# Delta rule's decay and step size rows: ten fp32 products with ones become twenty single-pass products on high and low parts

## The chip, the cores and the metric

The kernel runs on one core of a Trainium2 chip. The metric is the device time in microseconds of one execution; 955.31 us is the median of three runs of the kernel before. Names of engines: PE is TensorE, ACT is ScalarE, DVE is VectorE, POOL is GpSimd, SP is SyncE.

## The reference, cut to what matters

One inference step of one layer: a hybrid mixer (gated delta rule, a short convolution, stick-breaking attention), memory cross-attention and a convolutional feed-forward, for 512 prompt tokens and 8 samples of 16 tokens. The change lies in the gated delta rule. Of each chunk:

```python
gc = jnp.cumsum(g, axis=-1)
diff = gc[..., :, None] - gc[..., None, :]
decay = jnp.exp(jnp.where(causal, diff, -jnp.inf))
kk = jnp.einsum('bhtd,bhsd->bhts', k, k)
L = jnp.where(strict, beta[..., None] * kk * decay, 0.0)
qk = jnp.einsum('bhtd,bhsd->bhts', q, k) * decay
o = jnp.einsum('bhtk,bhkv->bhtv', q * jnp.exp(gc)[..., None], S) + ...
```

`diff` needs, for every token of a tile, the cumulated decay of every other token, and `L` the step size beta: values that stand one to a partition (a column) have to stand along the free dimension in every partition (a row).

## The kernel before

The 640 tokens are five tiles (NT) of 128: four of the prompt (PT = 4) and one of the eight samples. Each engine runs one program in order; semaphores tie them together. All the large weight products are already made from high and low parts in a format that PE handles in a single pass (F32R): `whi`, `wlo`, `hhi`, `hlo`; the small ones are fp32.

After the projections of q, k and v, each tile i goes through these steps.

- ACT, `decay_source(i)` (L1795): for each of four heads the triangle of ones is scaled by the decay `gdec` into `rsrc[i % 2][0]` (L1799), and the identity by the log of q's norm into `qdiag` (L1801).
- DVE, `query_norm(i)` (L2328): the sum of both, L2330.
- PE, `decay_rows(i)` (L780): two products with 4 columns (the cumulated decay as columns, bank gcol), then ones times `rsrc[..][0]`, 512 columns, L789: every partition gets the row of cumulated decays (bank grow).
- PE, `key_products(i)`: kk and qk, 128x128 for each head, L796.
- POOL, `beta_source(i)` (L1495): the identity times the step size `ratio`, L1498; PE, `beta_rows(i)`: ones times that, L803 (bank brow).
- DVE, `decay_part(i)`: small columns (L2364 to L2370), then the differences from bank grow (L2376); ACT takes two Exp (L1838 from DVE's differences, L1842 from the bank); POOL, `decays(i)`, masks with the triangle (L1485).
- DVE, in its loop: qk and kk times the decay (L2395, L2397), the next tile's `query_norm(i + 2)`, L times the beta row (L2402), q times its Exp (L2405), a transpose of the tile before (L2383).

PE's order is four fill units, `decay_rows(0)`, `key_products(0)`, `decay_rows(1)`, `beta_rows(0)`, and then for each tile i from 1: a fill unit, `decay_rows(i + 1)`, `key_products(i)`, `beta_rows(i)`. A fill unit is 24 single-pass products of 320 columns of another projection (L495 to L497), there to keep PE at work while the others prepare. ACT's order is `decay_source(0)`, an Exp for the ratio, `decay_source(1)`, `z_out(2)`, and then for each tile: small Exps, the two Exps, `decay_source(i + 2)`, `z_out(3 + i)` (a fill unit's bank to SBUF), `blocks_out(i - 1)`. The buffers of sources are two deep, so `decay_source(i + 2)` waits for L789 of tile i. After the last tile come the level products (L837, L843), which solve the triangular system.

Of the kernel before, what the change touches and what calls it, by code (L numbers as in the profile page):

```python
# [67 lines left out]
def hybrid_step(nc, A, O):  # L68
    ctx = ExitStack()
    with ctx:  # L70
        at_r5 = [R5]

        def at(name, shape, offset, dt=F32):
            return nc.alloc_sbuf_tensor_at(name, shape, dt, offset=offset)

        def keep(name, shape, dt=F32):
            n = 4
            for s in shape[1:]:
                n *= s
            t = at(name, shape, at_r5[0], dt)  # L80
            at_r5[0] += (n + 31) // 32 * 32
            return t
# [4 lines left out]
        def spread(ap, axis, shape):  # L87
            return ap.unsqueeze(axis).to_broadcast(shape)
# [35 lines left out]
        apart_q, apart_w = [at("apart_q", [P, 2, HEADS, P], R1), at("apart_w", [P, 2, HEADS, P], R1 + 2 * TILE)]  # L124
        smp_vn, smp_o = [at(f"smp{n}", [P, HEADS, P], R1 + TILE * (4 + n)) for n in range(2)]

        rsrc = [[at(f"rsrc{n}{m}", [P, HEADS, P], CQ + TILE * (2 * n + m)) for m in range(2)] for n in range(2)]

        sqG = [at(f"sqG{n}", [P, TOK], CQ + TOK * 4 * n) for n in range(2)]
        rG = [at(f"rG{n}", [P, TOK], KT + TOK * 4 * n) for n in range(2)]  # L130
# [66 lines left out]
        junk3 = at("junk3", [P, D_MODEL], at_r5[0] - 2 * 2688)  # L197
        ident = keep("ident", [P, P])
        ones = keep("ones", [P, P])
        uptri = keep("uptri", [P, P])  # L200
        up16 = keep("up16", [P, P])
        same16 = keep("same16", [P, P])
        same64 = keep("same64", [P, P])
        lmask = keep("lmask", [P, LEVELS, P])
        at_ones = at_r5[0] - (5 + LEVELS) * P * 4
        T_AT = {"gate": (R0, R0 + 6144), "up": (RF, at_ones)}
        traw = {n: at(f"traw_{n}", [P, 3, half_block, P], o[0]) for n, o in T_AT.items()}
        tlo = {n: at(f"tlo_{n}", [P, 3, half_block, P], o[0], F32R) for n, o in T_AT.items()}
# [15 lines left out]
        def lane(name, *dims):  # L224
# [16 lines left out]
        lnr = keep("lnr", [P, NT, HEADS, 2])  # L241
        pick = keep("pick", [P, 64])
        ratio = keep("ratio", [P, NT, HEADS])
        gown = keep("gown", [P, HEADS, DEC_BATCH])
        kdec = keep("kdec", [P, NT, HEADS])
        bege = keep("bege", [P, NT, HEADS])
# [17 lines left out]
            "eps_ready", "ident_ready", "consts", "small_loaded", "gains_loaded", "w_first", "w_first_lo", *[f"x_loaded{n}" for n in range(X_PARTS)], "ones_ready", "xhi_ready", "xlo_ready", "sqx_ready", "sqs_ready", "rx_ready",  # L264
            "hf_ready", "hhi_ready", "hlo_ready", "mrow_loaded", "memT_loaded", "mem_hi", "mem_lo", "mk_rstd", "pz_ready", "rstd_ready", "xn_ready", "h_hi_ready",
            "w_hi_ready", "w_lo_ready", "w_lo_dve", "w8_ready", "add4_ready", "kstep", "conv_done", "cq_zeros", "sig_ready", "silu_done", "sq_ready",
            "l2_ready", "ratio_act", "ratio_ready", "decay_row", "decay_src", "beta_src", "gates", "gates_act", "dif_ready", "dt_ready", "dtu_ready", "small_exp",
            "lt_ready", "xt0_ready", "xb_ready", "xt_zero", "lb_ready", "lm_ready", "kd_ready", *[f"v_cache_loaded{n}" for n in range(DEC_BATCH)],
            *[f"k_cache_loaded{n}" for n in range(DEC_BATCH)], "yb_ready", "apart_zero", "apart_ready", "A_ready", "q_blocks", "past_ready", "st_loaded", "vm_ready", "sqf_ready", "rf_ready", "y_ready",
            "yhi_ready", "ylo_ready", "xres_loaded", "gm_loaded", "f_loaded", "qroot_ready", "qscale_ready",  # L270
# [5 lines left out]
        def flat(t):  # L276
            return t[:, :, :].rearrange("p a b -> p (a b)")
# [28 lines left out]
        def tri(i):  # L306
            return uptri if i < PT else up16
# [122 lines left out]
        def _(pe):  # L430
# [12 lines left out]
            def done(ins, key):  # L443
                ins.then_inc(bank_full[use[key][0]], 1)
# [332 lines left out]
                    scores(scored)  # L777

            ring[0] = "gdn"
            def decay_rows(i):  # L780
                b = take(("gcol", i))
                T.matmul(bank[b][:, 0:4], (uptri if i < PT else up16)[:, :], gdec[:, i, :], start=True, stop=True)
                if i == PT:
                    T.matmul(bank[b][:, 8:8 + HEADS * DEC_BATCH], ones[:, :], flat(gown), start=True, stop=True)
                done(T.matmul(bank[b][:, 4:8], (ones if i < PT else same16)[:, :], gdec[:, i, :],
                              start=True, stop=True), ("gcol", i))
                pe.wait_ge(s["decay_src"], i + 1)
                b = take(("grow", i))
                done(T.matmul(bank[b][:, :], ones[:, :], flat(rsrc[i % 2][0]), start=True, stop=True), ("grow", i))  # L789

            def key_products(i):
                tt = slice(i * P, (i + 1) * P)
# [7 lines left out]
            def beta_rows(i):  # L800
                pe.wait_ge(s["beta_src"], i + 1)
                b = take(("brow", i))
                done(T.matmul(bank[b][:, :], ones[:, :], flat(rsrc[i % 2][1]), start=True, stop=True), ("brow", i))  # L803

            for n in range(4):
                fill()
# [579 lines left out]
        def _(pool):  # L1386
# [3 lines left out]
            def link(ins):  # L1390
                chain[0] += 1
                ins.then_inc(s["pool_chain"], 1)
                pool.wait_ge(s["pool_chain"], chain[0])
# [32 lines left out]
            for t, v in ((newm, 0.0), (own8, 1.0), (same16, 1.0)):  # L1426
# [15 lines left out]
                     channel_multiplier=-1))  # L1442
            sel(out=own8[:, :], in_=own8[:, :], compare_op=ALU.is_ge, fill=0.0, base=DEC_SEQ - 1,
                pattern=[[DEC_SEQ, DEC_BATCH]], channel_multiplier=-1)
            link(G.memset(pick[:, :], 0.0))
            G.memset(pick[:, 32:33], 1.0)
            G.tensor_copy(lmask[:, 0, :], ident[:, :])
# [47 lines left out]
            def beta_source(i):  # L1495
                if i >= 2:
                    filled(pool, ("brow", i - 2))
                G.tensor_tensor(rsrc[i % 2][1][:, :, :], spread(ident[:, :], 1, [P, HEADS, P]),  # L1498
                                spread(ratio[:, i, :], 2, [P, HEADS, P]), ALU.mult).then_inc(s["beta_src"], 1)

            pool.wait_ge(s["ratio_ready"], 1)
            filled(pool, ("z", NI - 1, 0))
            beta_source(0)
            beta_source(1)
            decays(0)
# [66 lines left out]
        def _(act_e):  # L1572
# [222 lines left out]
            def decay_source(i):  # L1795
                if i >= 2:
                    filled(e, ("grow", i - 2))
                for h in range(HEADS):
                    V(rsrc[i % 2][0][:, h, :], tri(i)[:, :], ACT.Copy, scale=gdec[:, i, h:h + 1])  # L1799
                for h in range(HEADS):  # L1800
                    ins = V(qdiag[i % 2][:, h, :], ident[:, :], ACT.Copy, scale=lnr[:, i, h, 0:1])  # L1801
                ins.then_inc(s["decay_row"], 1)

            evacuated(e, ("gates", 2))
            e.wait_ge(s["gates_act"], 1)
# [10 lines left out]
            e.wait_ge(s["l2_ready"], 1)  # L1816
            decay_source(0)
            V(ratio[:, :, :], ratio[:, :, :], ACT.Exp, scale=-0.5).then_inc(s["ratio_act"], 1)
            decay_source(1)
            z_out(2)  # L1820

            def blocks_out(i):
# [5 lines left out]
            for i in range(NT):  # L1828
                evacuated(e, ("gcol", i))
                V(kdec[:, i, :], gcs[:, i, 2, :], ACT.Exp)  # L1830
                V(bege[:, i, :], gcs[:, i, 3, :], ACT.Exp)
                if i < PT:
                    ins = V(etot[:, i, :], gcs[:, i, 1, :], ACT.Exp)
                else:
                    ins = V(etotS[:, :, :], etotS[:, :, :], ACT.Exp)
                ins.then_inc(s["small_exp"], 1)
                e.wait_ge(s["dif_ready"], i + 1)
                V(scr[4 + i % 2][:, :, :], scr[4 + i % 2][:, :, :], ACT.Exp).then_inc(s["dt_ready"], 1)  # L1838
                if i >= 2:
                    e.wait_ge(s["lt_ready"], i - 1)  # L1840
                b = filled(e, ("grow", i))
                V(scr[6 + i % 2][:, :, :], quad(b), ACT.Exp).then_inc(bank_free[b], 1)  # L1842
                if i + 2 < NT:
                    decay_source(i + 2)
                z_out(3 + i)
                if i >= 1:
                    blocks_out(i - 1)
                if i == 3:
                    cut_hi(B_SB)
            cut_hi(B_OUT[0][0])  # L1850
# [276 lines left out]
        def _(dve):  # L2127
# [199 lines left out]

            def query_norm(i):  # L2328
                dve.wait_ge(s["decay_row"], i + 1)
                V.tensor_tensor(rsrc[i % 2][0][:, :, :], rsrc[i % 2][0][:, :, :], qdiag[i % 2][:, :, :], ALU.add)                    .then_inc(s["decay_src"], 1)  # L2330

            for u, (name, i, c, h) in enumerate(UNITS):
                ct = (u - 8) // 2
# [14 lines left out]
                if h == 1 and ct >= 1:  # L2348
# [5 lines left out]
            query_norm(0)  # L2354
            dve.wait_ge(s["ratio_act"], 1)
            V.scalar_tensor_tensor(out=ratio[:, :, :], in0=ratio[:, :, :], scalar=DK ** 0.5, in1=beta[:, :, :],
                                   op0=ALU.mult, op1=ALU.mult).then_inc(s["ratio_ready"], 1)
            query_norm(1)
            dve.wait_ge(s["out_sb"], 64)

            passed(dve, ("av", NI - 1))
# [23 lines left out]
            decay_part(0)  # L2385
            for i in range(NT):
                tt = slice(i * P, (i + 1) * P)
                if i + 1 < NT:
                    decay_part(i + 1)
                dve.wait_ge(s["small_exp"], i + 1)  # L2390
                V.tensor_tensor(bege[:, i, :], bege[:, i, :], beta[:, i, :], ALU.mult)
                dve.wait_ge(s["dtu_ready"], i + 1)
                d = scr[8 + i % 2][:, :, :]
                b = filled(dve, ("qk", i))
                V.tensor_tensor(qkD[i][:, :, :], quad(b), d, ALU.mult).then_inc(bank_free[b], 1)  # L2395
                b = filled(dve, ("kk", i))
                V.tensor_tensor(LT[i][:, :, :], quad(b), d, ALU.mult).then_inc(bank_free[b], 1)  # L2397
                if i + 2 < NT:
                    query_norm(i + 2)
                evacuated(dve, ("kk", i))  # L2400
                b = filled(dve, ("brow", i))
                V.tensor_tensor(LT[i][:, :, :], LT[i][:, :, :], quad(b), ALU.mult).then_inc(bank_free[b], 1)  # L2402
                evacuated(dve, ("grow", i))
                er = scr[6 + i % 2]
                V.tensor_tensor(qkvz[:, 0:HEADS, tt], qkvz[:, 0:HEADS, tt], er[:, :, :], ALU.mult).then_inc(s["lt_ready"], 1)  # L2405
                if i == 3:
                    cut_lo(B_SB)
                if i >= 1:
                    turn_blocks(i - 1)
# [475 lines left out]
```

## Time and profile before

| | us |
|---|---|
| median of three runs | 955.31 |
| lowest and highest | 954.7, 955.76 |
| the profiled execution | 955.39 |
| its span on the core | 953.7 |
| PE busy in the span | 937.7 (98%) |
| DVE, ACT, POOL busy | 647.9, 451.9, 169.7 |

In a timeline a row's first number is the start in us from the span's start, the second the duration of the record; an engine's next instruction can start before the record of the one ahead has ended, so what an instruction costs its engine is the distance to the next start. One fp32 product leaves two records (x2). In brackets stands how long the engine had been idle and what released it.

### The profile page before, as it was taken

What the parts mean: (1) busy time and instruction counts of PE and PEld (TensorE: products, weight loads), DVE (VectorE), ACT (ScalarE), POOL (GpSimd) and SP (SyncE); (2) the same over time, 40 slices, a digit from 0 to 9 for tenths busy, and PEclk for the clock granted to TensorE, in tenths of its full rate; (3) what the DMA queues carried; (4) which work ended last, traced back from release to release, by engine and by line L of the source; (5) the groups of instructions that cost most, each with busy time, mean ns of one, the idle gap of its engine ahead of it and who ended that gap; (6) DMA issues with size and microseconds to landing.
All of it is one profiled execution on the core that took longest, in us unless ns stands there. A gap on an engine that the chain in (4) does not pass through costs nothing.

```text
span 953.7 us, 16664 instructions
## 1 busy us (share of the span) xinstructions
PE 937.7 (98%) x6807; PEld 848.9 (89%) x6807; DVE 647.9 (68%) x1083; ACT 451.9 (47%) x836; POOL 169.7 (18%) x198
## 2 busy tenths in 40 slices
PE   9999999999989999999999999999999999999998
PEld 8899888998868877889888999999999999888887
DVE  7627888776676455661665999999999999435321
ACT  6634454648466335463664345444444446333310
POOL 0061101104654241000001042222222220000000
PEclk9999999999999999999999999999999999999999
DMA  8624243221104066043822422222222223413221
GB/s 299 230 80 144 69 154 90 71 70 46 45 4 134 2 225 213 14 164 115 321 96 66 177 91 89 82 77 75 81 86 90 89 89 124 172 45 110 67 99 55
DMA packets 73820, 103.69 MB, mean 109 GB/s; under 512 B 2577, under 2 KB 53905, under 8 KB 73361
## 3 DMA queue, kind: packets, MB, share of 16 engines
q1 hardware_dynamic: 73744, 102.63, 32.2%
q8 instruction: 54, 0.88, 0.4%
q14 instruction: 22, 0.17, 0.1%
HBM read 92.27 MB, written 10.35 MB: 108 GB/s over the span
## 4 chain that ended last, share of the span: by engine, by line
PE 89%; DVE 5%; ACT 3%; issue 1%; POOL 1%; DMA 1%; SPq 0%; ACTq 0%; DVEq 0%; POOLq 0%
PE bank L1198 8%; PE bank L1199 8%; PE bank L1200 8%; PE bank L533 7%; PE bank L535 7%; PE bank L534 7%; PE bank L495 6%; PE bank L497 5%; PE bank L496 5%; PE bank L463 4%; PE bank L559 2%; PE bank L561 2%; PE bank L560 2%; PE bank L588 1%; PE bank L483 1%
## 5 line engine op out<-in xcount | busy, mean ns | idle before, releaser
L2141 DVE TENSOR_TENSOR wlo<-wraw,whi 128x2048 fp32r<-128x2048 f32 (+1 forms) x56 | 126.1, 2252 | 103.8 <-ACT whi L1591 94.5
L1591 ACT ACTIVATE whi<-wraw 128x2048 fp32r<-128x2048 f32 (+1 forms) x58 | 109.3, 1885 | 100.0 <-PE bank L535 72.9
L495 PE MATMUL bank<-hhi,whi 128*128 128x320 f32 x352 | 116.1, 330 | 0.0
L497 PE MATMUL bank<-hhi,wlo 128*128 128x320 f32 x352 | 108.7, 309 | 0.0
L496 PE MATMUL bank<-hlo,whi 128*128 128x320 f32 x352 | 108.7, 309 | 0.0
L495 PEld LDWEIGHTS bank<-hhi,whi 128*128 128x128 f32 x352 | 66.2, 188 | 4.7 <-issue 3.8
L496 PEld LDWEIGHTS bank<-hlo,whi 128*128 128x128 f32 x352 | 66.2, 188 | 2.8 <-issue 2.2
L497 PEld LDWEIGHTS bank<-hhi,wlo 128*128 128x128 f32 x352 | 66.1, 188 | 0.0
L533 PE MATMUL bank<-whi,hhi 128*128 128x512 f32 x150 | 58.4, 389 | 0.0
L534 PE MATMUL bank<-wlo,hhi 128*128 128x512 f32 x150 | 58.4, 389 | 0.0
L535 PE MATMUL bank<-whi,hlo 128*128 128x512 f32 x150 | 58.3, 389 | 0.0
L1559 POOL TENSOR_TENSOR traw_up<-wraw 128x512 f32<-128x512 f32 x10 | 14.3, 1432 | 196.2 <-PE bank L1200 170.6
L1198 PE MATMUL bank<-hhi,whi 128*128 128x320 f32 x152 | 47.1, 310 | 0.0
L1200 PE MATMUL bank<-hhi,wlo 128*128 128x320 f32 x152 | 47.0, 309 | 0.0
L1198 PE MATMUL bank<-shi,whi 128*128 128x320 f32 x152 | 47.0, 309 | 0.0
L1199 PE MATMUL bank<-slo,whi 128*128 128x320 f32 x152 | 47.0, 309 | 0.0
L1200 PE MATMUL bank<-shi,wlo 128*128 128x320 f32 x152 | 47.0, 309 | 0.0
L1199 PE MATMUL bank<-hlo,whi 128*128 128x320 f32 x152 | 47.0, 309 | 0.0
L463 PE MATMUL bank<-hhi,whi 128*128 128x320 f32 x128 | 38.7, 310 | 1.1 <-DVE wlo L2141 1.1
L463 PE MATMUL bank<-hlo,whi 128*128 128x320 f32 x128 | 38.5, 309 | 0.0
L2516 DVE TENSOR_TENSOR xres<-xres,bank 128x512 f32<-128x512 f32 x30 | 20.1, 684 | 26.4 <-PE bank L535 18.8
L2239 DVE SCALAR_TENSOR_TENSOR act<-cb,flanes,act 128x512 f32<-128x512 f32 x44 | 33.0, 749 | 0.9
(489 smaller groups left out, 2684.3 us busy)
## 6 DMA issues: line engine op xcount, KB each, us to landing
wraw<-in_w_in SPq DMA_DIRECT2D x13, 1024.0 KB, 5.3
wraw<-in_w_gate SPq DMA_DIRECT2D x11, 1024.0 KB, 5.2
wraw<-in_w_up SPq DMA_DIRECT2D x11, 1024.0 KB, 5.2
wraw<-in_w_down SPq DMA_DIRECT2D x10, 1024.0 KB, 5.1
kTs<-in_cache_sb_k SPq DMA_DIRECT2D x8, 512.0 KB, 4.5
vraw<-in_cache_sb_v SPq DMA_DIRECT2D x8, 512.0 KB, 5.0
wraw<-in_w_mix_out SPq DMA_DIRECT2D x4, 1024.0 KB, 6.0
kmT<-in_cache_mem_k SPq DMA_DIRECT2D x8, 512.0 KB, 6.1
```

Of the source, the lines that this page charges most:

```text
L463: ins = T.matmul(bank[bs[h]][:, 0:HALF], w[:, k, c * P:(c + 1) * P], a[:, k, h * HALF:(h + 1) * HALF], start=(k == 0 and w is wh and a is hi),
L495: T.matmul(o, wh[:, k, cs], hhi[:, k, hs], start=(k == 0), stop=False)
L496: T.matmul(o, wh[:, k, cs], hlo[:, k, hs], start=False, stop=False)
L497: ins = T.matmul(o, wl[:, k, cs], hhi[:, k, hs], start=False, stop=(k == KD - 1))
L533: T.matmul(o, hi[:, t * P:(t + 1) * P], wh[:, kk, :], start=(k == 0), stop=False)
L534: T.matmul(o, hi[:, t * P:(t + 1) * P], wl[:, kk, :], start=False, stop=False)
L535: ins = T.matmul(o, lo[:, t * P:(t + 1) * P], wh[:, kk, :], start=False, stop=(k == nk - 1))
L1198: T.matmul(o, w[0][:, k, :], a[0][:, k, :], start=(k == 0), stop=False)
L1199: T.matmul(o, w[0][:, k, :], a[1][:, k, :], start=False, stop=False)
L1200: ins = T.matmul(o, w[1][:, k, :], a[0][:, k, :], start=False, stop=(k == half_block - 1))
L1591: V(wv(whi, i), wv(wraw, i), ACT.Copy).then_inc(s["w_hi_ready"], 1)
L2141: V.tensor_tensor(wv(wlo, i), wv(wraw, i), wv(whi, i).bitcast(F32), ALU.subtract)\
```

## The change

The sources of the decay row and of the beta row are each split into a high part in the single-pass format and the rest, the low part. PE then makes two single-pass products with ones (`ones_r`, a rounded copy of the ones) in place of one fp32 product; both add up in the same bank. For the decay row, ACT writes the raw source to `rraw`, DVE adds `qdiag` to it, ACT rounds the sum to `rhi` (`decay_hi`), DVE subtracts to `rlo` (`decay_lo`). For the beta row, the small `ratio` is split once, 20 columns (ACT and DVE), and POOL multiplies the identity with both parts, two instructions a tile. `decay_hi(0)` and the ratio's copy stand before `decay_source(1)` on ACT, `decay_hi(i + 2)` at the end of its iteration; `decay_lo(i + 1)` stands at the head of DVE's iteration. POOL waits once more, for the last value product of the attention, since two of the new buffers lie where its operands were.

```diff
+        ones_r = keep("ones_r", [P, P], F32R)
...
+            def row_sums(b, i, m, key):
+                T.matmul(bank[b][:, :], ones_r[:, :], flat(rhi[i % 2][m]), start=True, stop=False)
+                done(T.matmul(bank[b][:, :], ones_r[:, :], flat(rlo[i % 2][m]), start=False, stop=True), key)
...
-                done(T.matmul(bank[b][:, :], ones[:, :], flat(rsrc[i % 2][0]), start=True, stop=True), ("grow", i))
+                row_sums(b, i, 0, ("grow", i))
...
-                done(T.matmul(bank[b][:, :], ones[:, :], flat(rsrc[i % 2][1]), start=True, stop=True), ("brow", i))
+                row_sums(b, i, 1, ("brow", i))
...
+            G.tensor_copy(ones_r[:, :], ones[:, :])
...
-                G.tensor_tensor(rsrc[i % 2][1][:, :, :], spread(ident[:, :], 1, [P, HEADS, P]),
-                                spread(ratio[:, i, :], 2, [P, HEADS, P]), ALU.mult).then_inc(s["beta_src"], 1)
+                for out, r in ((rhi, ratio_hi), (rlo, ratio_lo)):
+                    ins = G.tensor_tensor(out[i % 2][1][:, :, :], spread(ident[:, :], 1, [P, HEADS, P]),
+                                          spread(r[:, i, :].bitcast(F32), 2, [P, HEADS, P]), ALU.mult)
+                ins.then_inc(s["beta_src"], 1)
...
+            passed(pool, ("av", NI - 1))
...
-                    V(rsrc[i % 2][0][:, h, :], tri(i)[:, :], ACT.Copy, scale=gdec[:, i, h:h + 1])
+                    V(rraw[i % 2][:, h, :], tri(i)[:, :], ACT.Copy, scale=gdec[:, i, h:h + 1])
...
+            def decay_hi(i):
+                e.wait_ge(s["decay_sum"], i + 1)
+                V(rhi[i % 2][0][:, :, :], rraw[i % 2][:, :, :], ACT.Copy).then_inc(s["decay_hi"], 1)
...
             V(ratio[:, :, :], ratio[:, :, :], ACT.Exp, scale=-0.5).then_inc(s["ratio_act"], 1)
+            decay_hi(0)
+            e.wait_ge(s["ratio_sum"], 1)
+            V(ratio_hi[:, :, :], ratio[:, :, :], ACT.Copy).then_inc(s["ratio_hi"], 1)
             decay_source(1)
+            decay_hi(1)
             z_out(2)
...
                 if i >= 1:
                     blocks_out(i - 1)
+                if i + 2 < NT:
+                    decay_hi(i + 2)
...
+            def decay_lo(i):
+                dve.wait_ge(s["decay_hi"], i + 1)
+                V.tensor_tensor(rlo[i % 2][0][:, :, :], rraw[i % 2][:, :, :], rhi[i % 2][0][:, :, :].bitcast(F32), ALU.subtract)\
+                    .then_inc(s["decay_src"], 1)
...
+            decay_lo(0)
+            dve.wait_ge(s["ratio_hi"], 1)
+            V.tensor_tensor(ratio_lo[:, :, :], ratio[:, :, :], ratio_hi[:, :, :].bitcast(F32), ALU.subtract)\
+                .then_inc(s["ratio_ready"], 1)
             query_norm(1)
+            decay_lo(1)
...
             for i in range(NT):
                 tt = slice(i * P, (i + 1) * P)
+                if 2 <= i + 1 < NT:
+                    decay_lo(i + 1)
                 if i + 1 < NT:
                     decay_part(i + 1)
```

## Rows read from the trace of the kernel before

**Rows 1.** page, parts 1 and 2: busy us (share); busy tenths in 40 slices

```profile
PE 937.7 (98%) x6807; PEld 848.9 (89%) x6807; DVE 647.9 (68%) x1083; ACT 451.9 (47%) x836; POOL 169.7 (18%) x198
...
PEclk9999999999999999999999999999999999999999
```

**Rows 2.** waits of PE: waited for: us in total, times, longest

```profile
PE bank L1198 <- DVE tlo_gate L2696: 1.1, 1, 1.1
```

**Rows 3.** chain that ended last: start us, us, what

```profile
225.49 0.86 PE bank L803 x2
...
230.21 0.96 PE bank L789 x2
...
231.17 1.78 PE bank L796 x16
```

**Rows 4.** windows: stretch, length, busy (count) of PE, PEld, DVE, ACT, POOL

```profile
233.65:241.12 7.47, 7.47 (x50) 6.51 (x48) 5.86 (x16) 5.04 (x17) 6.55 (x8) 1.00 0.01 2
```

**Rows 5.** timeline of PE: start us, us, line, op, shapes, xcount

```profile
9.78 0.40 PE L533 MATMUL bank<-whi,xhi 128*128 128x512 f32 x1
...
10.01 0.39 PE L534 MATMUL bank<-wlo,xhi 128*128 128x512 f32 x1
```

**Rows 6.** timeline of ACT, same columns

```profile
218.87 1.27 ACT L1799 ACTIVATE rsrc<-uptri,gdec 128x128 f32<-128x128 f32 x4
...
221.22 0.41 ACT L1709 ACTIVATE qkvz<-bank 128x320 f32<-128x320 f32 x1
...
224.35 0.58 ACT L1842 ACTIVATE scr<-bank 128x512 f32<-128x512 f32 x1
...
224.83 1.26 ACT L1799 ACTIVATE rsrc<-uptri,gdec 128x128 f32<-128x128 f32 x4
```

**Rows 7.** page, part 5: groups; busy us, mean ns; idle before

```profile
L2141 DVE TENSOR_TENSOR wlo<-wraw,whi 128x2048 fp32r<-128x2048 f32 (+1 forms) x56 | 126.1, 2252 | 103.8 <-ACT whi L1591 94.5
...
L1591 ACT ACTIVATE whi<-wraw 128x2048 fp32r<-128x2048 f32 (+1 forms) x58 | 109.3, 1885 | 100.0 <-PE bank L535 72.9
```

**Rows 8.** timeline of DVE

```profile
218.89 0.69 DVE L2330 TENSOR_TENSOR rsrc<-rsrc,qdiag 128x512 f32<-128x512 f32 x1 [2.60 <-ACT qdiag L1801]
...
219.50 0.17 DVE L2356 SCALAR_TENSOR_TENSOR ratio<-ratio,beta 128x20 f32<-128x20 f32 x1
...
221.34 1.00 DVE L2330 TENSOR_TENSOR rsrc<-rsrc,qdiag 128x512 f32<-128x512 f32 x1 [1.67 <-ACT qdiag L1801]
...
222.27 0.15 DVE L2364 TENSOR_TENSOR gcs<-bank,lnr 128x4 f32<-128x4 f32 x1
...
234.27 1.15 DVE L2330 TENSOR_TENSOR rsrc<-rsrc,qdiag 128x512 f32<-128x512 f32 x1
```

**Rows 9.** timeline of POOL

```profile
219.76 2.04 POOL L1498 TENSOR_TENSOR rsrc<-ident,ratio 128x512 f32<-128x512 f32 x2 [30.18 <-DVE ratio L2356]
...
224.52 1.27 POOL L1485 TENSOR_TENSOR scr<-scr,uptri 128x512 f32<-128x512 f32 x1 [2.72 <-ACT scr L1838]
...
233.83 1.04 POOL L1498 TENSOR_TENSOR rsrc<-ident,ratio 128x512 f32<-128x512 f32 x1
...
234.83 1.19 POOL L1492 TENSOR_TENSOR lmb<-LTb,lmask 128x256 f32<-128x256 f32 x1
```

**Rows 10.** timeline of PE, decay rows and the first level product

```profile
224.38 1.10 PE L789 MATMUL bank<-rsrc,ones 128*128 128x512 f32 x2
...
229.70 0.28 PE L782 MATMUL bank<-gdec,uptri 128*128 128x4 f32 x2
...
230.06 1.10 PE L789 MATMUL bank<-rsrc,ones 128*128 128x512 f32 x2
...
258.58 1.15 PE L837 MATMUL bank<-Xb,lmb 64*64 64x64 f32 x32
```

**Rows 11.** timelines of DVE and PE: a wait of PE on DVE

```profile
262.85 0.45 DVE L2383 STREAM_TRANSPOSE Xb<-XTb 128x256 f32<-128x256 f32 x1
...
263.40 0.27 PE L837 MATMUL bank<-Xb,lmb 64*64 64x64 f32 x2 [0.63 <-DVE Xb L2383]
```

More of the change, by code:

```diff
@@ L125, in hybrid_step @@
         smp_vn, smp_o = [at(f"smp{n}", [P, HEADS, P], R1 + TILE * (4 + n)) for n in range(2)]
-        rsrc = [[at(f"rsrc{n}{m}", [P, HEADS, P], CQ + TILE * (2 * n + m)) for m in range(2)] for n in range(2)]
+        rhi = [[at(f"rhi{n}{m}", [P, HEADS, P], CQ + TILE * (2 * n + m), F32R) for m in range(2)] for n in range(2)]
+        RLO = ((CQ + 4 * TILE, R0), (RF + 3 * TILE, R0 + 2 * TILE))
+        rlo = [[at(f"rlo{n}{m}", [P, HEADS, P], RLO[n][m], F32R) for m in range(2)] for n in range(2)]
+        rraw = [at(f"rraw{n}", [P, HEADS, P], RLO[n][0]) for n in range(2)]
         sqG = [at(f"sqG{n}", [P, TOK], CQ + TOK * 4 * n) for n in range(2)]
@@ L204, in hybrid_step @@
         lmask = keep("lmask", [P, LEVELS, P])
-        at_ones = at_r5[0] - (5 + LEVELS) * P * 4
+        at_ones = at_r5[0] - (6 + LEVELS) * P * 4
         T_AT = {"gate": (R0, R0 + 6144), "up": (RF, at_ones)}
@@ L243, in hybrid_step @@
         ratio = keep("ratio", [P, NT, HEADS])
+        ratio_hi, ratio_lo = [keep(f"ratio_{n}", [P, NT, HEADS], F32R) for n in ("hi", "lo")]
         gown = keep("gown", [P, HEADS, DEC_BATCH])
@@ L266, in hybrid_step @@
             "w_hi_ready", "w_lo_ready", "w_lo_dve", "w8_ready", "add4_ready", "kstep", "conv_done", "cq_zeros", "sig_ready", "silu_done", "sq_ready",
-            "l2_ready", "ratio_act", "ratio_ready", "decay_row", "decay_src", "beta_src", "gates", "gates_act", "dif_ready", "dt_ready", "dtu_ready", "small_exp",
+            "l2_ready", "ratio_act", "ratio_sum", "ratio_hi", "ratio_ready", "decay_row", "decay_sum", "decay_hi", "decay_src", "beta_src", "gates", "gates_act", "dif_ready", "dt_ready", "dtu_ready", "small_exp",
             "lt_ready", "xt0_ready", "xb_ready", "xt_zero", "lb_ready", "lm_ready", "kd_ready", *[f"v_cache_loaded{n}" for n in range(DEC_BATCH)],
@@ L2329, in query_norm @@
                 dve.wait_ge(s["decay_row"], i + 1)
-                V.tensor_tensor(rsrc[i % 2][0][:, :, :], rsrc[i % 2][0][:, :, :], qdiag[i % 2][:, :, :], ALU.add)                    .then_inc(s["decay_src"], 1)
+                V.tensor_tensor(rraw[i % 2][:, :, :], rraw[i % 2][:, :, :], qdiag[i % 2][:, :, :], ALU.add).then_inc(s["decay_sum"], 1)
+            def decay_lo(i):
+                dve.wait_ge(s["decay_hi"], i + 1)
+                V.tensor_tensor(rlo[i % 2][0][:, :, :], rraw[i % 2][:, :, :], rhi[i % 2][0][:, :, :].bitcast(F32), ALU.subtract)\
+                    .then_inc(s["decay_src"], 1)
             for u, (name, i, c, h) in enumerate(UNITS):
@@ L2356, in _ @@
             V.scalar_tensor_tensor(out=ratio[:, :, :], in0=ratio[:, :, :], scalar=DK ** 0.5, in1=beta[:, :, :],
-                                   op0=ALU.mult, op1=ALU.mult).then_inc(s["ratio_ready"], 1)
+                                   op0=ALU.mult, op1=ALU.mult).then_inc(s["ratio_sum"], 1)
+            decay_lo(0)
+            dve.wait_ge(s["ratio_hi"], 1)
+            V.tensor_tensor(ratio_lo[:, :, :], ratio[:, :, :], ratio_hi[:, :, :].bitcast(F32), ALU.subtract)\
+                .then_inc(s["ratio_ready"], 1)
             query_norm(1)
+            decay_lo(1)
             dve.wait_ge(s["out_sb"], 64)
```

## The prediction

> **What bounds the kernel now.** I read the page's busy times first: TensorE (PE) is busy for 937.7 of 953.7 us, VectorE (DVE) for 647.9, and the granted clock is full in every slice, 2.4 GHz [rows 1]. The list of waits says the same from the other side: the longest single wait of PE within the span is 1.1 us [rows 2]. The chain that ended last, read for the stretch of the change (221 to 255 us), holds PE's products alone, L785, L789, L796, L803 and the fill units [rows 3]. So today each us less of PE work there is a us less of span. Whether that stays so depends on DVE, ScalarE (ACT) and GpSimd (POOL), which feed these products. In the iteration from 233.65 to 241.12 (7.47 us) DVE is busy 5.86 us, POOL 6.55 and ACT 5.04 [rows 4]: the cover is thin.
>
> **PE's part, a gain.** Removed are ten fp32 products of 512 columns: five decay rows (L789) and five beta rows (L803). In the chain one of L803 takes 0.86 us and one of L789 takes 0.96 us, from start to next start [rows 3]. Added are twenty single-pass products of the same 512 columns; the projection's own single-pass products start 0.23 us apart (9.78, 10.01) [rows 5], so a pair takes 0.46 us. That saves 0.40 us at a beta row and 0.40 to 0.50 us at a decay row; 10 x 0.40 = 4.0 us is the value I take, because the extra 0.10 us at L789 may be what changing over to the small products beside it costs and then stays. The end at 5.0 us (0.50 each) needs everything in favour. This is the whole gain that can be had.
>
> **What it adds on the other engines.** Per tile: a ScalarE cut to the high part and a DVE subtraction for the low part, each 128x512, and a second GpSimd product. The nearest rows: ACT's Exp over 128x512 takes 0.48 us from start to next start (224.35 to 224.83) [rows 6]; the same kind of cut on 128x2048 has a mean of 1885 ns, a quarter of it 0.47 [rows 7]; I take 0.52, the upper of the two and a little for the start. DVE's sum over 128x512 takes 0.69 us in the record and 0.61 from start to next start (218.89 to 219.50); the low cut of 128x2048 has a mean of 2252 ns, a quarter of it 0.56 [rows 7, 8]; I take 0.60. GpSimd's beta source takes 1.02 us each, 2.04 for two [rows 9]; its double is another 1.0.
>
> **Where it stands in the queues, which is what decides.** A decay source was: ACT scales eight blocks, DVE adds, PE may go. Now it is ACT, DVE, ACT, DVE, and both engines are in order. I carry every queue forward with the durations of the rows, 0.03 us from one engine to the next.
>
> Start. DVE's first sum ends at 219.58 [rows 8]. Before, ACT was by then already scaling the second source, from 218.87 [rows 6]. Now it first waits for that sum, cuts (0.52) and copies the ratio (0.1), and starts the second source at 220.2: 1.35 us late. The first low part is there at 220.9, PE comes for it at 221.3: hidden, with 0.4 us to spare. The second source takes 2.35 us (218.87 to 221.22 [rows 6]), so to 222.6. Sum (0.85 beside GpSimd; before it stood at 1.00 in the record against 0.69 [rows 8]), high cut, low cut: ready at 225.1. PE, which is 0.4 us early, comes at 224.0. **Wait 1.1 us.** Queued behind this low cut on DVE is the whole chain of tile 0, whose first piece (L2364, 222.27 [rows 8]) moves to 225.0: 2.7 us late.
>
> Tile 2. Behind DVE's piece are ACT's two Exp of tile 0, which ended at about 224.83, when the third source began [rows 6]; they now end at 227.6. The source takes 2.35, to 229.95. DVE's sum starts at 230.1, as soon as the source is there. ACT cuts at 230.8 to 231.3, while DVE goes through two more products of 0.60, and only then, at the head of its next iteration, makes the low part: 231.9 to 232.5. PE is at this product at 225.1 + 0.54 + 0.46 (decay row with its 0.08 of overhead, beta row) + 3.52 (fill unit; 226.18, where L803's 0.86 ends, to 229.70 without the change) + 0.36 (the 4-column products) = 230.0; before it ran it at 230.06 [rows 10]. **Wait 2.6 us.**
>
> Tiles 3 and 4. PE needs 7.47 - 0.80 = 6.67 us for an iteration. DVE, from one low cut to the next: small ones 0.42, wait 0.42 for the decay row, 1.04 for the differences, 0.07, wait 0.65 for the qk product (behind the decay row on PE), six of 0.60, transpose 0.36 = 6.6, and about 1.0 of waiting for GpSimd, whose product now goes twice: 7.6. So DVE sets the pace and PE **waits 1.0 and 0.9 us** more. No decay row is left after tile 4, and the last two beta rows give their 0.8 undisturbed.
>
> **Sum.** Waits 1.1 + 2.6 + 1.0 + 0.9 = 5.6; I add 0.07 for each, as PE starts 0.10 after DVE's transpose ends (263.30 to 263.40 [rows 11]) and I used 0.03: 5.9. Less 4.0 saved: +1.9 us. Against the profiled execution's 955.39 us that is 957.3; the median of 955.31 lies 0.08 below it, which is nothing here. What follows (level products, states) starts from PE's fill unit and its chains are the same, so it moves as one piece; I find nothing that gives it back, as all later waits of PE are short ones on work that PE itself started. The rest costs nothing: the copy of the ones on GpSimd is 200 us early; its added wait for the last value product is long met; its later start (219.76 to about 221.0 [rows 9]) still has the first beta source ready at 223.1, PE comes after 225.
>
> **A rule that bears on it.** The trace: GpSimd's product from 233.83 makes DVE's sum of 234.27 take 1.15 us in place of 0.69, and GpSimd's next then takes 1.19 at 234.83 [rows 8, 9]; each holds the other off, rather than both being slower a little. The Trainium skill, page SBUF — State Buffer, section Who interferes with whom, says that the pair of ports which VectorE and GpSimd share is an exclusive lock, and that a VectorE instruction with two SBUF inputs contends with a GpSimd instruction that reads SBUF. By that rule, the trace agrees, both the sum and the low cut queue with the doubled beta source. Without any such waits my walk ends at -0.6 us, with them at +1.9.
>
> **Rivals.**
> - B, the port decides more. If GpSimd's product with rounded output takes 1.3 us, not 1.0 (its decay product over the same shape stands at 1.27 [rows 9]), every DVE sum and low cut waits longer and the loop grows by 0.5 to 1.0 us over three tiles: +3.2 to +4.3, 958.6 to 959.7. For it: 6.55 of 7.47 us busy on GpSimd already [rows 4]. Chance 0.15.
> - C, the other side: faster. The source chain is hidden. It decides at one point, whether the low part is there before PE has finished the fill unit ahead of it. That needs DVE to reach the low cut of tile 2 before 230.0, 2.5 us sooner than I have it. Then the full 4.0 to 5.0 us stand: 950.4 to 951.4. Against it: ACT's 1.35 us at the start are certain from the program's order. Chance 0.08.
> - D, half hidden: start-up waits as above, but DVE and GpSimd interleave well and tiles 3 and 4 catch up: -0.6 to +0.9, 954.8 to 956.3. Chance 0.18.
> - E, the clock. PE stands for 2.6 us with only a few 4-column products ahead; no row shows a wait beyond 1.1 us, so nothing here excludes that the grant falls to 1.2 GHz, half of the granted 2.4 GHz of today's rows [rows 1]; the next fill unit would then take, as an estimate, twice its 3.52 us: +1.9 + 3.5 = +5.4, 960.8. Chance 0.05. (The Trainium skill, page TensorE: Matmul & The Clock Gate, section What's actually happening, has the clock throttled by default and released by activity; no run here shows it after such a wait.)
> - F, the pair of single passes costs nearly as much as fp32 did, from changing over between kinds. Where PE waits anyway that is partly hidden; it ends within B's times. Chance 0.03.
>
> **How the numbers follow.** The forecast case (957.3, its own range 956.4 to 958.5) has 0.51. A measurement of this kernel tells about 0.2%, 1.9 us, from no change, which cuts this case in the middle: 0.28 slower, 0.23 same. D goes to same (0.18), B, E and F to slower (0.23), C to faster (0.08): faster 0.08, same 0.41, slower 0.51. The range leaves out C and E: 954.8 from D's end to 959.7 from B's.
>
> **What would show it.** Right: in the list of waits, PE's new longest wait is at the decay row's product behind DVE's low cut, some 2.6 us at tile 2, four such in all with 5 to 6 us together; ACT's second source starts at about 220.2; DVE's first small piece of tile 0 at about 225.0; the pairs start 0.23 us apart; the level products begin near 260.4, against 258.58 [rows 10]. Wrong: the level products begin before 257, or PE's waits at the decay rows are under 4 us together; then the walk of the queues fails, at the first row that is early. If waits are over 7 us, it is GpSimd's price.

## The result and the profile after

The changed kernel takes 957.02 us (median of 20, 955.24 to 958.70) against 955.32 us before (20, 954.44 to 955.76): a ratio of 1.0017, interval 1.0010 to 1.0024, so slower by 1.7 us. Its profiled execution took 957.49 us with a span of 955.8 us (before: 955.39 and 953.7). The forecast was 957.3. The sum came out near; two of its parts did not, and they nearly cancel. In the profiled execution they are a clock that fell (+1.6 us) and 1.2 us given back 320 us later. To that extent it is luck that the time came out near.

Busy times of the changed kernel, from its page (engine, us, share, instructions), to be set beside [rows 1]: PE's busy time is 2.9 us less, DVE's 6.5 more.

```profile
PE 934.8 (98%) x6807; PEld 849.7 (89%) x6807; DVE 654.4 (68%) x1089; ACT 454.5 (48%) x842; POOL 178.2 (19%) x204
```

The list of PE's waits of the changed kernel (engine, what it waited for: us in total, times, longest). First in it is a wait that did not exist, at the decay row's product (now L786) behind DVE's low cut (L2357); the wait of [rows 2], PE's on `tlo_gate`, is gone from the list. A wait on `xlo` near 9 us is longer (1.9 us, before 0.9), but PE's products ahead of it end 1.1 us sooner; at the 4-column products of tile 0 PE is 0.08 us ahead of the kernel before (220.85 against 220.93), so nothing comes in from there.

```profile
PE bank L786 <- DVE rlo L2357: 5.1, 4, 2.4
```

PE's timeline in the changed kernel (start, us, engine, line, operation, [idle before <- who ended it]): tile 1's decay row and tile 0's beta row, tile 2's decay row, tile 1's key products and the start of its beta row, tile 3's decay row and the first level product, to be read against [rows 3] and [rows 10].

```profile
225.15 0.50 PE L786 MATMUL bank<-rhi,ones_r 128*128 128x512 f32 x1 [1.11 <-DVE rlo L2357]
225.49 0.40 PE L787 MATMUL bank<-rlo,ones_r 128*128 128x512 f32 x1
225.73 0.39 PE L786 MATMUL bank<-rhi,ones_r 128*128 128x512 f32 x1
225.96 0.39 PE L787 MATMUL bank<-rlo,ones_r 128*128 128x512 f32 x1
...
229.70 0.28 PE L791 MATMUL bank<-gdec,uptri 128*128 128x4 f32 x2
229.84 0.36 PE L794 MATMUL bank<-gdec,ones 128*128 128x4 f32 x2
232.60 0.50 PE L786 MATMUL bank<-rhi,ones_r 128*128 128x512 f32 x1 [2.40 <-DVE rlo L2357]
232.94 0.39 PE L787 MATMUL bank<-rlo,ones_r 128*128 128x512 f32 x1
233.17 3.57 PE L805 MATMUL bank<-qkvz 128*128 128x128 f32 x16
236.39 0.58 PE L786 MATMUL bank<-rhi,ones_r 128*128 128x512 f32 x1
...
241.90 0.50 PE L786 MATMUL bank<-rhi,ones_r 128*128 128x512 f32 x1 [0.83 <-DVE rlo L2357]
...
262.06 1.15 PE L846 MATMUL bank<-Xb,lmb 64*64 64x64 f32 x32
```

Behind another pair, the two products of a pair start 0.23 us apart (225.73, 225.96); behind fp32 products it is 0.31 to 0.34. The four waits stand where the prediction put them. One line has no counterpart there: the sixteen key products (L805) behind the 2.40 us wait take 3.22 us to the next start, against 1.78 in [rows 3]. The view by stretches of the changed kernel (stretch, its length, busy time of PE, PEld, DVE, ACT and POOL, granted clock, DMA share, GB/s) says why:

```profile
229.70:233.17 3.47, 1.07 (x8) 0.90 (x7) 3.07 (x9) 3.03 (x11) 0.88 (x1) 1.00 0.00 0
233.17:236.39 3.22, 3.22 (x17) 3.22 (x16) 1.19 (x5) 2.91 (x10) 0.74 (x2) 0.51 0.00 0
236.39:237.04 0.65, 0.65 (x5) 0.57 (x4) 0.19 (x1) 0.00 (x0) 0.57 (x2) 0.82 0.00 0
237.04:241.80 4.76, 4.02 (x29) 3.93 (x27) 4.76 (x8) 2.51 (x9) 4.76 (x5) 1.00 0.01 3
```

In the 3.5 us before, PE was busy for 1.07; then the grant stands at 0.51, the 1.2 GHz level, for the key products, and is back at 2.4 GHz by 237.04. The price is 3.22 - 1.70 (these products' start-to-start time behind a single-pass pair at full clock, as at 242.46 and 250.30) plus 0.65 - 0.54 for the beta pair behind them: 1.6 us.

The ACT and DVE timelines of the changed kernel carry the walk's three dates:

```profile
220.18 1.27 ACT L1812 ACTIVATE rraw<-uptri,gdec 128x128 f32<-128x128 f32 x4
```

```profile
224.35 0.75 DVE L2357 TENSOR_TENSOR rlo<-rraw,rhi 128x512 fp32r<-128x512 f32 x1 [0.69 <-ACT rhi L1819]
225.02 0.15 DVE L2397 TENSOR_TENSOR gcs<-bank,lnr 128x4 f32<-128x4 f32 x1
...
231.87 0.68 DVE L2357 TENSOR_TENSOR rlo<-rraw,rhi 128x512 fp32r<-128x512 f32 x1
...
236.85 0.69 DVE L2430 TENSOR_TENSOR qkD<-bank,scr 128x512 f32<-128x512 f32 x1 [2.28 <-PE bank L805]
```

ACT begins the second source at 220.18, DVE's first small piece of tile 0 starts at 225.02, tile 2's low cut at 231.87; foreseen were 220.2, 225.0 and 231.9. The last line is the slow key products again, seen from DVE.

**Where 1.2 us come back.** At the level products the changed kernel is 3.48 us behind (262.06 against 258.58 [rows 10]), at the end of the span only 2.1. Laying PE's two timelines side by side, the distance falls by more than 0.2 us for good at one place alone, in the first gate block of the feed-forward stage: from 3.27 us at the last products ahead of it (577.35 and 580.62) to 2.11 behind it. Before:

```profile
577.35 0.41 PE L1198 MATMUL bank<-hhi,whi 128*128 128x320 f32 x1
...
577.51 1.30 POOL L1559 TENSOR_TENSOR traw_up<-wraw 128x512 f32<-128x512 f32 x1 [15.94 <-PE bank L1200]
577.73 2.70 DVE L2696 TENSOR_TENSOR tlo_gate<-traw_gate,thi_gate 128x1536 fp32r<-128x1536 f32 x1
580.48 0.41 PE L1198 MATMUL bank<-shi,thi_gate 128*128 128x320 f32 x1 [1.11 <-DVE tlo_gate L2696]
```

and in the changed kernel:

```profile
580.62 0.31 PE L1207 MATMUL bank<-hhi,whi 128*128 128x320 f32 x1
...
580.78 1.76 DVE L2731 TENSOR_TENSOR tlo_gate<-traw_gate,thi_gate 128x1536 fp32r<-128x1536 f32 x1
580.93 2.77 POOL L1572 TENSOR_TENSOR traw_up<-wraw 128x512 f32<-128x512 f32 x1 [17.54 <-PE bank L1209]
582.59 0.41 PE L1207 MATMUL bank<-shi,thi_gate 128*128 128x320 f32 x1
```

Before, POOL's difference starts 0.22 us ahead of DVE's low cut; the cut then takes 2.70 us and PE waits 1.11. After, DVE is 0.15 us ahead; its cut takes 1.76, POOL's takes 2.77 in place of 1.30, and PE, which needs DVE's result and not POOL's, does not wait. POOL has moved by 3.42 us and DVE by 3.05; these 0.37 us turn the order.

### The profile page after: what moved, and what is told of

Its sections match the earlier page's. It is cut to its first block, busy times and chain, and to the rows that moved or that the text cites. A ratio compares the mean times of both kernels' runs of the same rounds, so it can differ in the third digit from the quotient of the medians.

```text
span 955.8 us, 16682 instructions
## 1 busy us (share of the span) xinstructions
PE 934.8 (98%) x6807; PEld 849.7 (89%) x6807; DVE 654.4 (68%) x1089; ACT 454.5 (48%) x842; POOL 178.2 (19%) x204
## 4 chain that ended last, share of the span: by engine, by line
PE 84%; DVE 9%; ACT 4%; issue 2%; POOL 1%; DMA 1%; SPq 0%; DVEq 0%; ACTq 0%
PE bank L1207 8%; PE bank L1209 8%; PE bank L1208 8%; PE bank L538 7%; PE bank L540 7%; PE bank L539 7%; PE bank L468 4%; PE bank L500 4%; PE bank L502 4%; PE bank L501 4%; PE bank L564 2%; PE bank L566 2%; PE bank L565 2%; DVE wlo L2164 1%; PE bank L593 1%
```

## The experiments

All ratios are to the kernel before on the same chip; of each edit the lines that matter are shown. For each execution there is also the mean granted clock over the whole span: 0.998 means that some 0.2% of 955 us was lost to the clock, about one such fall of 1.6 us. For the changed kernel the 20 executions divide by it: at 1.000 stand 5, from 955.24 to 955.96 us; at 0.998 stand 13, from 956.43 to 958.13; at 0.996 stand 2, 957.44 and 958.70. Of the 27 and 23 executions of the kernel before beside the experiments, one in each has 0.998 (956.46 and 957.54): without the new wait a fall is rare, but not unknown. Where in an execution the clock fell is seen only in a profiled one; for the others it is inferred.

**1. Keep PE at work while it waits.** The waits are filled with single-pass products whose result the decay row's own product overwrites.

```
+                b = take(("grow", i))
+                for _ in range({1: 4, 2: 10, 3: 3, 4: 3}.get(i, 0)):
+                    T.matmul(bank[b][:, :], ones_r[:, :], hhi[:, 0, 0:512], start=True, stop=True)
                 pe.wait_ge(s["decay_src"], i + 1)
-                b = take(("grow", i))
```

> The changed kernel, and ahead of each wait for a decay source from tile 1 on PE makes single-pass products of 512 columns that nobody reads (4, 10, 3 and 3 of them, 0.23 us each), into the bank that it fills afterwards. They fill the waits that the trace of the changed kernel shows (1.1, 2.4, 0.8, 0.8 us) and put off nothing. Theory clock: in the profiled execution of the changed kernel the granted clock is 0.51 from 233.17 to 236.39, just behind the wait of 2.4 us, and 16 records of key products there take 3.2 us where they took 1.8; without an idle PE the clock stays whole, the key products take 1.8 us again, and the time is 1.6 us under the changed kernel's 957.0: 955.4, with a spread as narrow as that of the kernel before. Rival, waits alone: the time stays at 957.0 +- 0.3 and as wide, since PE still waits for the same sources.

Measured: 955.35 us (954.5 to 955.75), ratio 0.9996 (0.9987 to 1.0005). No execution of 11 has a clock under 0.999. PE's timeline of this kernel at tile 2, and its first level product:

```profile
230.31 2.56 PE L798 MATMUL bank<-hhi,ones_r 128*128 128x512 f32 x10
232.86 0.50 PE L786 MATMUL bank<-rhi,ones_r 128*128 128x512 f32 x1
233.20 0.39 PE L787 MATMUL bank<-rlo,ones_r 128*128 128x512 f32 x1
233.42 1.95 PE L807 MATMUL bank<-qkvz 128*128 128x128 f32 x16
235.13 0.48 PE L786 MATMUL bank<-rhi,ones_r 128*128 128x512 f32 x1
...
260.56 1.15 PE L848 MATMUL bank<-Xb,lmb 64*64 64x64 f32 x32
```

The decay row starts no earlier (232.86 against 232.60), yet the key products are back at 1.71 us (233.42 to 235.13). So the wait itself stays and the clock's price goes: level products 1.98 us behind the kernel before, not 3.48. The kernel's median is then 1.7 us under that of the changed one, although PE does more, and the intervals of the two ratios don't overlap.

**2. Fill only the long wait.** As 1, with ten products at tile 2 alone.

```
-                for _ in range({1: 4, 2: 10, 3: 3, 4: 3}.get(i, 0)):
+                for _ in range({2: 10}.get(i, 0)):
```

> As e_warm, but only the longest wait is filled: ten single-pass products that nobody reads, ahead of the wait for tile 2's decay source; the waits of tiles 1, 3 and 4 (1.1, 0.8, 0.8 us) stay empty. If the long wait of 2.4 us is what lets the clock fall, the clock stays whole in every execution and the time is e_warm's 955.4. If several shorter waits add up to it, the clock falls in part of the executions and the median lies between 955.4 and 957.0, with a spread of 2 us and more.

Measured: 955.59 us (954.9 to 955.99), ratio 1.0001 (0.9992 to 1.0010), and in none of 10 executions does the clock fall. PE's waits at this product:

```profile
PE bank L786 <- DVE rlo L2359: 2.8, 3, 1.2
```

The three waits that are left, up to 1.2 us, cost no clock; with the one of 2.40 the clock fell in 15 of 20 executions.

**3. The decay rows alone.** The beta rows stay one fp32 product on one POOL source.

```
-                row_sums(b, i, 1, ("brow", i))
+                done(T.matmul(bank[b][:, :], ones[:, :], flat(rbeta[i % 2]), start=True, stop=True), ("brow", i))
```

> Only the decay rows go to single passes; the beta rows stay one fp32 product from one GpSimd source. PE saves 2.0 us in place of 4.0. My walk of the queues, with this taken in: waits at the decay rows of 1.1, 2.2, 0.6 and 0.2 us, 4.0 together, level products 2.0 us behind the kernel before if the clock stays whole, and 1.6 more in executions in which it falls behind the longest wait. Theory chain: as slow as the changed kernel or slower, 955.7 to 957.5, the source chain carries the loss. Rival, GpSimd's doubled source is what makes the waits: then they nearly vanish here and the time is 953.3.

Measured: 956.83 us (955.36 to 958.72), ratio 1.0015 (1.0006 to 1.0024). Its waits, longest 2.01 us at tile 2:

```profile
PE bank L787 <- DVE rlo L2356: 3.4, 3, 2.0
```

With POOL's work not doubled the wait is still there and the time is that of the whole change, so the chain of sum, high cut and low cut carries the loss. What the doubling adds is in the later waits: 0.32 us here at tile 3 and none at tile 4, against 0.83 and 0.77. The clock falls in 7 of 10 executions here, and the longest wait is 2.0 us. The profiled one (955.89 us) is not among the seven: its clock stays full behind the 2.01 us, so it is inferred from experiment 2, and not seen, that the falls of the others lie there. Its first level product starts at 260.78, 2.20 us behind the kernel before; 2.0 were expected.

**4. The beta rows alone.** The decay rows stay one fp32 product of DVE's sum; the ratio is split on DVE.

```
-                row_sums(b, i, 0, ("grow", i))
+                done(T.matmul(bank[b][:, :], ones[:, :], flat(rraw[i % 2]), start=True, stop=True), ("grow", i))
```

> Only the beta rows go to single passes; the decay rows stay fp32 from DVE's sum, the ratio is split on DVE, GpSimd makes two sources a tile. Nothing is put between the sum and PE. By the same walk of the queues: no wait at any row, five pairs save 0.40 us each, level products at 256.6 in place of 258.58. Time 953.4, or 952.4 if DVE also comes first at the port at 577 us. Rival, GpSimd's doubled source holds up DVE: level products after 257.5 and waits at the decay rows, 954.5 or more.

Measured: 952.27 us (951.92 to 953.06), ratio 0.9970 (0.9958 to 0.9981): **the best kernel with the whole computation, 3.1 us under before.** PE has no wait at these rows. The first level product:

```profile
257.27 1.15 PE L846 MATMUL bank<-Xb,lmb 64*64 64x64 f32 x32
```

That is 1.31 us before that of [rows 10], where 5 x 0.39 = 2.0 were saved; a fill unit that comes too early for a cut of weights (a wait of 0.42 us on `wlo` at 253.56) takes most of the rest. At the gate block DVE's cut starts at 575.85, 1.88 us before that of the kernel before, and POOL's difference at 576.01: DVE is first again, and PE's product, at 577.66, is 2.82 ahead of 580.48. So this kernel holds the gain at the second place as well: of its 3.1 us about 1.2 are the order at the gate block, and experiment 6 gets 1.0 from that order without any change at the rows. The beta rows themselves are worth the rest, about 2.

**5. No chain at all.** From 4: DVE's sum is written in the rounded form itself, and PE reads it twice. The kernel leaves out the low part and adds the high part twice, so its decays are not those of the reference.

```
-                V.tensor_tensor(rraw[i % 2][:, :, :], rraw[i % 2][:, :, :], qdiag[i % 2][:, :, :], ALU.add).then_inc(s["decay_src"], 1)
+                V.tensor_tensor(rsum[i % 2][:, :, :], rraw[i % 2][:, :, :], qdiag[i % 2][:, :, :], ALU.add).then_inc(s["decay_src"], 1)
```

> Leaves out the decay row's low part: DVE's sum is written at once in the single-pass format, and PE's second product of the pair reads the same high part again, so the decays are wrong (doubled). PE's twenty single-pass products stay, the beta rows' two parts stay (the ratio is split on DVE), but neither ACT's cut nor DVE's subtraction stands between the sum and PE. Prediction's theory: the gain of the products alone is 4.0 us at the level products (254.6 instead of 258.58) and no wait at the decay rows is left; if nothing later gives or takes, 951.4. Rival: the pairs cost more than 0.46 us behind fp32 products, gain under 3 us. Second rival: GpSimd's doubled beta source alone makes DVE late, and PE waits at the decay rows for the sum all the same.

Measured: 950.99 us (950.49 to 951.12), ratio 0.9951 (0.9937 to 0.9964), span 948.8. PE's timeline: decay rows of tiles 2 and 3, first level product.

```profile
229.00 0.48 PE L799 MATMUL bank<-rsum,ones_r 128*128 128x512 f32 x1
229.32 0.40 PE L800 MATMUL bank<-rsum,ones_r 128*128 128x512 f32 x1
...
235.67 0.48 PE L799 MATMUL bank<-rsum,ones_r 128*128 128x512 f32 x1
...
255.44 1.15 PE L848 MATMUL bank<-Xb,lmb 64*64 64x64 f32 x32
```

An iteration is 235.67 - 229.00 = 6.67 us, just what the prediction had for PE undisturbed (7.47 - 0.80), and the level products come 3.14 us early. Of the 4.0 us saved the last fill unit gives back 0.7, of which 0.43 is a wait on a cut of weights (`wlo`, at 251.72), and PE came to tile 0 0.12 late. So the pairs do save what the prediction said, and what the changed kernel pays is the chain. Of the 4.5 us in the median some 1.2 are again the order at the gate block (DVE's cut at 573.78, POOL at 573.95).

**6. The order at the port, before.** In the kernel before, POOL's difference is made to come after DVE's cut.

```
+                if kind == "up" and j == 2:
+                    pool.wait_ge(s["tlo_gate"], 1)
```

> The kernel before, with one wait more: GpSimd's first difference of weights for up block 2 waits until DVE has written its first tlo_gate. In the trace of before GpSimd starts at 577.51, DVE's tlo_gate at 577.73 takes 2.70 us and PE waits 1.1 us for it; in the trace of the changed kernel DVE is first (580.78 against 580.93), takes 1.76 and PE does not wait; there the two kernels' distance falls from 3.4 to 2.1 us. Theory port: letting DVE go first gives 1.3 us by itself: 954.0. Rival: GpSimd, now later, delays ACT's next high cut and the gain is lost: 955.3.

Measured: 954.45 us (953.58 to 955.57), ratio 0.9989 (0.9981 to 0.9998). At the gate block:

```profile
576.83 1.76 DVE L2698 TENSOR_TENSOR tlo_gate<-traw_gate,thi_gate 128x1536 fp32r<-128x1536 f32 x1
578.75 1.29 POOL L1561 TENSOR_TENSOR traw_up<-wraw 128x512 f32<-128x512 f32 x1 [18.10 <-DVE tlo_gate L2698]
578.64 0.42 PE L1198 MATMUL bank<-shi,thi_gate 128*128 128x320 f32 x1 [0.17 <-DVE tlo_gate L2698]
```

DVE's cut is 1.76 us with POOL held back, and 1.0 us of the median goes without any change at the decay rows (by the interval of the ratio 0.2 to 1.8). (In this execution PE came to the place 0.9 us earlier as well; that has another cause, told last.)

**7. The old order in the warm kernel.** Experiment 1, and DVE's first gate cut waits until POOL's difference is done.

```
+                if kind == "gate" and j == 2:
+                    dve.wait_ge(s["pool_first"], 1)
```

> e_warm, and in the first feed-forward block DVE's first tlo_gate waits until GpSimd has made its first difference for up block 2: the order that the kernel before has by itself (577.51 ahead of 577.73). In e_warm's own trace DVE is first (579.05 against 579.20) and the distance to the kernel before falls there from 1.54 to 0.39 us. Theory: the changed kernel's gain at this place is only that turn of order; with the order put back the sum of my prediction stands without it, 955.35 + 1.2 = 956.5, 1.1 to 1.5 over the kernel before. Rival: the 1.15 us are given back by something else, slack that PE has there in any case; then the time stays at 955.4.

Measured: 957.39 us (957.18 to 959.19), ratio 1.0029 (1.0020 to 1.0038), 2.0 us over experiment 1; expected was 956.5. PE's product at the gate block:

```profile
582.43 0.41 PE L1209 MATMUL bank<-shi,thi_gate 128*128 128x320 f32 x1 [2.58 <-DVE tlo_gate L2737]
```

The direction holds, the size does not: the forced wait ends only behind POOL's instruction, so DVE starts 1.4 us behind POOL, not 0.2, and PE waits 2.58 us, not 1.11. This kernel shows that a late gate cut costs time: 1.9 of the 2.58 us, by the five executions at full clock (957.18 to 957.39) against experiment 1. It does not measure the price of the natural order. And it bears on the clock: with this one wait added, in another stage, the clock falls in 4 of 9 executions (958.52 to 959.19), where it fell in none of 11. The profiled execution (957.30) is one of the five whose clock stays full behind the wait, so the place of the falls is inferred here too.

**8. The order made sure in the beta kernel.** Experiment 4 with the wait of 6.

```
+                if kind == "up" and j == 2:
+                    pool.wait_ge(s["tlo_gate"], 1)
```

> e_beta_only with the one wait of e_port_before (GpSimd's first difference for up block 2 after DVE's first tlo_gate), which was worth 1.0 us there. If the two gains are of separate places they add: 955.4 - 2.0 - 1.0 = 952.4. If e_beta_only already turns the order at the port by itself, both kernels give the same time.

Measured: 952.48 us (952.04 to 952.80), ratio 0.9968 (0.9956 to 0.9979), the same as 4: there the order had turned already.

## Why the prediction came out, and where it did not

- **PE's gain, 4.0 us: right.** Key products plus beta pair take 1.70 + 0.54 us in the changed kernel where they took 1.79 + 0.86: 0.41 saved; a decay pair takes 0.57 (232.60 to 233.17) in place of 0.96 or 0.94: 0.38. Ten of them are 3.9 to 4.0. The first product of a pair behind an fp32 one takes 0.31 to 0.34 to the next start, not 0.23, but the key products then take 0.08 less. Rival F falls: experiment 5 keeps these pairs and an iteration takes the 6.67 us foreseen.
- **The start-up walk: right** in its dates, to 0.1 us: ACT's second source 220.18 (220.2), wait 1.11 (1.1), DVE's piece 225.02 (225.0), cut of tile 2 at 231.87 (231.9), wait 2.40 (2.6 foreseen, of which 0.14 lie in the end of the 4-column products, which the list does not count). One step of it does not add up as written: 222.6 with 0.85, 0.52, 0.60 and three times 0.03 is 224.7, where 225.1 stands. The trace has the sum at 1.00 (222.65), the cut at 0.63 (223.69) and the low cut at 0.75 (224.35), and PE starts at 225.15: the next engine waits for the end of a record, 0.63, and not for the distance to the next start, 0.52. So the date is right, but the terms written for it are 0.4 us short.
- **Tiles 3 and 4: right**, 0.83 and 0.77 for 1.0 and 0.9, again less that 0.14; from low cut to low cut DVE takes 7.52 us (240.99 to 248.51) for the 7.6 foreseen. The waits are 5.1 us; with 0.14 each they are 5.7, where the sum had 5.9. Experiment 1, without the clock's part, has its level products 1.98 us behind where +1.9 was foreseen (260.56 for "near 260.4"), and PE's start at tile 0 takes 0.16 of it.
- **The clock: wrong.** Rival E named it and its place, the 2.6 us wait, but gave it a chance of 0.05 and a price of 3.5 us; the sum has it at nothing. A fall is recorded in 15 of 20 executions, and in the profiled one it costs 1.6: the estimate doubled a whole fill unit, while the grant was back within 3.9 us, in which only the key products and the beta pair lie. The Trainium skill, page TensorE: Matmul & The Clock Gate, section What's actually happening, has the clock throttled by default and released by activity; experiments 1 and 2 agree with that, as products put into the wait, whose results nobody reads, keep the grant at 0.999 or more in all 21 executions.
- **"What follows gives nothing back": wrong, by 1.2 us.** [rows 2] held the clue: PE's wait of 1.1 us at L1198 was priced at its length and called a wait on work that PE itself started. It was the price of DVE losing a race by 0.22 us. A wait behind a contended port isn't a fixed cost; it goes or comes when the two arrive by a few tenths otherwise.
- **Sum.** In the profiled execution 3.48 us at the level products, less 0.2 on the way, less 1.16 at the gate block, is +2.1 in the span; +1.9 was foreseen. A term put at nothing (the clock, +1.6) and a gain denied (the order at the port, -1.2) nearly cancel, and that is luck. With the clock at full grant the changed kernel's median is 955.42 (5 executions, 955.24 to 955.96), 0.1 over the kernel before, where the walk's +1.9 less the port's 1.2 would be +0.7. What takes the other 0.6 is not shown; the waits with no releaser told at the end differ by up to 0.9 us between single profiles. So the measured +1.7 has the size of the clock's part alone (957.02 less 955.42 is 1.6), and the walk's +1.9, which the trace shows up to the level products, is for the most part hidden in the time.
- **Rivals.** B falls: the rounded product takes POOL 1.04 us (221.07), and up to 1.49 only where DVE is at the port too, and the waits at tiles 3 and 4 are not longer than foreseen. (B's price doesn't follow from its words either: 0.5 to 1.0 us on +1.9 is +2.4 to +2.9, and three times that +3.4 to +4.9, not +3.2 to +4.3.) C's gain is real where PE need not wait, as experiment 5 shows with no low part to wait for, but its condition fails: the low cut of tile 2 starts at 231.87. D fits the executions with full clock in time, but not in cause, as tiles 3 and 4 did not catch up.

## What to carry to other kernels

Here a cheaper instruction on the bounding engine was paid for with a longer chain between other engines. Where that is so, before counting the gain, walk that chain through every in-order queue, and make only the half of the change whose sources have slack (here the beta rows, about -2 us, -3.1 with the order at the port; the decay rows cost what they save). Price each hand-over of the chain with the whole record, not with the distance to the next start. A new wait of TensorE of 2 us or more should be priced with the clock behind it (here 1.6 us, not in every execution), and can be filled with products whose result is thrown away. When two kernels drift apart or together far from the edit, look there for two engines that reach the shared port within a few tenths of a us of each other.

## What the runs showed of the hardware

- TensorE's grant fell to its 1.2 GHz level behind a wait of 2.40 us that had only the 4-column products in front of it, and stood there for the 3.2 us of the key products, in the one trace that shows a fall. By the mean clock of the executions it fell in 15 of 20 with this wait, in 7 of 10 where the longest wait at the rows was 2.01 us, in 4 of 9 with one of 2.58 us, in 0 of 10 where the waits at the rows were 1.2 us or less, in 0 of 11 where all of them were filled, and in 2 of 50 of the kernel before. In two executions of the changed kernel and two of experiment 3 the mean is 0.996, which is about two falls; where the second lies is open.
- A long wait does not make it fall each time: the traces of experiments 3 and 7 have waits of 2.01 and 2.58 us and a full clock behind them. What decides it the runs do not show.
- One lead of 0.15 to 0.22 us at the port of DVE and POOL decides which of two instructions takes 1 us more (DVE 1.76 or 2.70, POOL 1.30 or 2.77). Small DVE operations beside it show the same: POOL's beta source takes 1.04 us at 221.07 and 1.49 at 223.06, beside DVE's sum.
- The 0.37 us by which DVE and POOL came nearer to each other between the two kernels come from an earlier meeting of the same kind near 551 us, in which POOL comes 0.3 us sooner behind the same PE product in the kernels made from the changed one (its idle time there is 25.24 or 25.25 us, before 25.54). Why is open.
- In the level products PE has in some profiles a wait with no releaser, up to 0.9 us (0.9 in that of before, 0.7 in that of after, 0.6 in experiment 1, 0.9 in experiment 8, none in experiments 2 and 6). Two single profiles can't be told apart below that; the medians can.
